# Moving the first weight sums from GpSimd to VectorE, and using four gathered experts before the second tile's norm

## The reference

```python
def first_block(...):                                    # DEPTH = 1
    proj = rms_norm(h, g_mix_pre) @ w_in                 # conv, pool, u, v, and three gates
    z_sgu, z_conv, z_pool, z_gate = jnp.split(proj, SPLITS, axis=-1)
    br_a = spatial_gating(gelu(z_sgu), ...) @ w_sgu_out  # layer_norm of v, then a mix over tokens
    br_b = conformer_conv(z_conv, ...) @ w_conv_out      # a * sigmoid(gate), 31 taps, layer_norm, silu
    br_c = multiscale_pool(z_pool, ...) @ w_pool_out
    gates = sigmoid(z_gate).reshape(bsz, s, 3, D_MODEL)
    merged = gates[:, :, 0] * br_a + gates[:, :, 1] * br_b + gates[:, :, 2] * br_c
    h = h + rms_norm(merged @ w_out, g_mix_post)
    ...                                                  # feed-forward layer, embedding gate

def second_block(...):
    for i in range(2):
        h = layer_norm_2(DN_ALPHA * h + mix(h), ln_mix_g[i], ln_mix_b[i])
        h = layer_norm_2(DN_ALPHA * h + peer_ffn(h, ...), ln_ffn_g[i], ln_ffn_b[i])

def peer_ffn(x, w_q, sub_keys, u, v):                    # 128 tokens at a time
    q = (xb @ w_q).reshape(128, 8, 2, 128)               # 8 heads
    s1, i1 = lax.top_k(q . sub_keys[:, 0], 16)
    s2, i2 = lax.top_k(q . sub_keys[:, 1], 16)
    top_s, pos = lax.top_k(s1[:, None] + s2[None, :], 16)
    eidx = (i1 * 128 + i2) at pos                        # 16 experts per token and head
    h = gelu(einsum('thkd,td->thk', u[eidx], xb))
    return einsum('thk,thkd->td', softmax(top_s) * h, v[eidx])
```

## Time and profile before

| what | value |
|---|---|
| median of 3 runs | 2305.41 us (2303.39 to 2305.59) |
| the profiled execution's own time | 2303.99 us |
| its span | 2302.3 us |
| PE busy | 2074.8 us, 90% of the span |
| DVE busy | 1433.8 us, 62% |
| ACT busy | 697.5 us, 31% |
| POOL busy | 725.1 us, 31% |
| bytes moved | 703.05 MB |

### The profile page before, as it was taken

The page is one execution under the profiler, slowest core; times in us unless marked ns, Lnnn a source line. Parts: engine busy times, 40 slices in busy tenths (PEclk is TensorE's granted clock), DMA queues, the critical chain, the costliest instruction groups (busy, mean ns, idle before and its releaser), DMA issues.

```text
span 2302.3 us, 21846 instructions
## 1 busy us (share of the span) xinstructions
PE 2074.8 (90%) x6098; PEld 1096.2 (48%) x6098; DVE 1433.8 (62%) x3220; ACT 697.5 (30%) x1511; POOL 725.1 (31%) x641
## 2 busy tenths in 40 slices
PE   9989999999999999999887787889999989777876
PEld 8854455454876655444332222367544534222222
DVE  3997757675363336666666666532666666666664
ACT  1112102110200214334443434424334344343442
POOL 0274340000000004445544444400244544444442
PEclk9999999999999999999999999999999999999999
DMA  5434443444445249999999999973699999999997
GB/s 227 146 128 166 163 156 132 174 169 167 182 151 222 85 156 388 422 421 421 422 421 422 422 422 422 421 289 103 257 421 422 421 421 422 421 422 422 422 422 323
DMA packets 98441, 703.05 MB, mean 305 GB/s; under 512 B 11136, under 2 KB 11648, under 8 KB 13248
## 3 DMA queue, kind: packets, MB, share of 16 engines
q0 software_dynamic: 73856, 537.17, 56.2%
q1 hardware_dynamic: 20880, 147.33, 17.6%
q10 hardware_dynamic: 3632, 17.63, 2.1%
HBM read 700.51 MB, written 1.05 MB: 305 GB/s over the span
## 4 chain that ended last, share of the span: by engine, by line
PE 42%; DMA 30%; ACT 5%; issue 5%; DVE 3%; POOL 1%; POOLq 0%; DVEq 0%; ACTq 0%
DMA arena<-uv,expert_index 30%; PE aux L978 12%; PE acc L556 10%; PE acc L521 6%; PE aux L521 4%; PE aux L831 4%; PE acc L901 2%; PE acc L988 1%; ACT arena L1511 1%; ACT arena L1514 1%; ACT L1511 1%; POOL arena L1247 1%; ACT L1503 1%; DVE arena L2220 1%; PE acc L878 0%
## 5 line engine op out<-in xcount | busy, mean ns | idle before, releaser
L978 PE MATMUL aux<-arena 128*128 128x512 f32 x2048 | 1006.1, 620 | 186.0 <-ACT arena L1514 181.7
L1247 POOL DMA_INDIRECT arena<-uv,expert_index x512 | 589.2, 1151 | 1000.1 <-PE aux L978 612.2
L2220 DVE SCALAR_TENSOR_TENSOR arena<-arena 128x1024 f32<-128x1024 f32 x512 | 634.1, 1239 | 425.5 <-DMA arena<-uv,expert_index 424.9
L978 PEld LDWEIGHTS aux<-arena 128*128 128x128 f32 x2048 | 366.3, 192 | 725.5 <-ACT arena L1514 438.8
L1511 ACT ACTIVATE arena<-ident,dots 128x128 f32<-128x128 f32 x512 | 205.2, 401 | 702.8 <-DVE arena L2220 700.3
L556 PE MATMUL acc<-x,w_ring 128*128 128x256 f32 x1264 | 277.4, 382 | 5.1 <-DVEq L1957 2.7
L556 PEld LDWEIGHTS acc<-x,w_ring 128*128 128x128 f32 x1264 | 241.8, 192 | 39.6 <-issue 3.4
L1514 ACT ACTIVATE arena<-arena,gate 128x128 f32<-128x128 f32 x512 | 205.5, 401 | 17.0
L1743 DVE TENSOR_TENSOR first_query_weights<-w_ring 128x1024 f32<-128x1024 f32 (+1 forms) x63 | 76.1, 1207 | 106.3 <-PE aux L521 102.2
L521 PE MATMUL acc<-first_query_weights,arena 128*128 128x512 f32 (+1 forms) x268 | 133.4, 580 | 0.0
L1719 DVE SCALAR_TENSOR_TENSOR arena<-arena,channel_vectors x240 | 115.4, 562 | 0.2
(11 more groups left out here) (328 smaller groups left out, 1846.5 us busy)
## 6 DMA issues: line engine op xcount, KB each, us to landing
w_ring<-stream SPq DMA_DIRECT2D x139, 1024.0 KB, 4.8
arena<-uv,expert_index POOLq DMA_INDIRECT x512, 14.8
first_query_weights<-first_heads ACTq DMA_DIRECT2D x4, 1024.0 KB, 8.5
row_vectors<-rows ACTq DMA_DIRECT2D x3, 1024.0 KB, 12.4
scratch<-keys ACTq DMA_DIRECT2D x2, 1024.0 KB, 6.3
arena<-ret_out_held ACTq DMA_DIRECT2D x2, 1024.0 KB, 15.4
x<-first_heads ACTq DMA_DIRECT2D x2, 1024.0 KB, 4.8
arena<-rows ACTq DMA_DIRECT2D x1, 1024.0 KB, 4.7
```

The lines of the kernel that those rows point to most:

```text
L978: last = nc.tensor.matmul(AUX[2 * tt + c][:, :], DG[:, slot, :], G[:, row(slot), D + c * 512:D + (c + 1) * 512], start=False, stop=closes)
L1247: pool.indirect_dma_start(G[:, row(s), :], None, uv, bass.IndirectOffsetOnAxis(ap=EIDX[:, par, s:s + 1], axis=0),).then_inc(gathered[s % R ...
L2220: v.scalar_tensor_tensor(G[:, row(slot), 0:D], G[:, row(slot), 0:D], 1.0, HTM[:, tt, :], ALU.mult, ALU.mult, accum_out=HD[:, slot:slot + 1 ...
```

## The change

It has three parts.

1. In the first block the weight sums of unit 0 go from POOL to DVE. The last two rounds of taps are no longer a loop; in the last round three `combine(0, j)` stand before tap 8, 16 and 24, and the fourth stands behind it. POOL makes the sums of the normed input (`split(X1, ...)`) before its pooling work instead of after it, in another region (63 in place of 17), and no longer makes weight sums. Its sums of the pooled branch wait for unit 0's four steps, and those of the convolution go to a region of their own (17). The first `norm_values` goes from ahead of `combine(1, 0)` to behind `combine(1, 3)`, the second to behind `combine(BRANCH, 1)`. In the last merge one part of four stays on POOL and three are DVE's (two and two before).
2. In both expert layers four slots (`FIRST`) of the first unit are used ahead: DVE makes their dots before `mixer_norm(1)`, ACT their weights before the root of that norm, PE their products before the third head's early query. Places of `G` are given anew. In layer 1 seven gathers need no wait for the projection. In layer 0 the gathers 4, 5 and 6 wait for a part of it each (`rows_left`), and the order of that projection is turned round so that those parts come first; the weight slots of the blocks 113 and 114 are given back later in it. The next searches' pieces are spread over the twelve slots that are left, two a slot at first.
3. In layer 0 the fourth head's query weights (1 MB) come by an ACT transfer into tiles 72 to 79 (`Q3W`), after the retention's last heads are scaled, and no longer by the stream, which is one block shorter; its query steps stand two a slot behind slots 4 to 7.

```diff
+FIRST = 4
-          ... ("peer_q0", 5),
+          ... ("peer_q0", 4),
-        def row(s):
-            return (s + 2) % RING
+        def row(layer, s):
+            return s if layer else (2, 3, 4, 5, 7, 0, 1, 6)[s]
...
 @@ PE, seven_step
-                        if unit:
-                            pe.wait_ge(combined, step - STEPS + 1)
-                        else:
-                            pe.wait_ge(combined_pool, step + 1)
+                        pe.wait_ge(combined, step + 1)
 @@ PE, peer
+                        if kt == 16 and (c, k) in ((1, 15), (0, 3), (0, 7)):
+                            last.then_inc(rows_left, 1)
+                        elif not rest:
+                            last.then_inc(projected, 1)
...
+                if kt == 16:
+                    last.then_inc(w_free[(base + 1) % SLOTS], 1)
+                for s in range(FIRST):
+                    weigh_slot(layer, 0, s, layer * (PEER_SLOTS + 1) + 1 + s + 1)
                 pe.wait_ge(third_loaded, 16 * (layer + 1))
...
-                 [(1, k) for k in range(2, 8)] + [(0, k) for k in range(8)] + [(1, k) for k in range(8, 16)])
+                 [(1, k) for k in range(8, 16)] + [(0, k) for k in range(8)] + [(1, k) for k in range(2, 8)])
 @@ POOL, gathers
-                            if par == 0 and s == RING // 2:
+                            if par == 0 and layer == 0 and 4 <= s < RING - 1:
+                                pool.wait_ge(rows_left, s - 3)
+                            if par == 0 and s == RING - 1:
                                 pool.wait_ge(projected, TT * (layer + 1))
 @@ ACT
             gain_heads(3)
+            act.dma_start(Q3W, first_heads[2 * EARLY]).then_inc(fourth_loaded, 16)
...
                 exps(0, units0 + 1, None)
+                for s in range(FIRST):
+                    slot_weights(0, s, None)
                 root(RT)
 @@ DVE, first block
+                for k in range(CONV):
+                    if k in between:
+                        chain.wait_back(0)
+                        combine(0, between[k])
...
-            with repeat(dve, 2, (chain, 2 * CONV)) as i:
-                taps(i * 2 + 4)
+            taps(4)
+            taps(6, {8: 0, 16: 1, 24: 2})
+            combine(0, 3)
 @@ DVE, peer
+                for s in range(FIRST):
+                    slot_dots(0, 0, s, None)
                 mixer_norm(1)
```

More of the change, by code:

```diff
@@ L996, in experts @@
                 for u in range(HEADS):
-                    for s in range(TOPK):
-                        weigh_slot(0, s, base + u * TOPK + s + 1, u == HEADS - 1 and s == TOPK - 1)
+                    for s in range(0 if u else FIRST, TOPK):
+                        weigh_slot(layer, 0, s, base + u * TOPK + s + 1, u == HEADS - 1 and s == TOPK - 1)
                         if 1 <= u <= HEADS - AHEAD and s == 2:
@@ L1003, in experts @@
                         if u < HEADS - AHEAD:
-                            for k in range(3) if u and s == 2 else () if u and s < 2 else (s,):
-                                query_step(k)
+                            two = 2 * (s - FIRST)
+                            for k in range(3) if u and s == 2 else () if u and s < 2 else \
+                                    (two, two + 1) if u == 0 and s < 2 * FIRST else (s,):
+                                query_step(k, layer == 0 and u == 0)
                         else:
@@ L1214, in _ @@
                 merge(1, *part)
-            for part in PARTS[:2]:
-                merge(2, *part)
+            merge(2, *PARTS[0])
             pool.wait_ge(input_ready, 4)
@@ L1350, in _ @@
             gates(2)
+            root(RT)
             for u in range(3):
@@ L1537, in peer @@
                 for unit in range(HEADS):
-                    for s in range(TOPK):
+                    for s in range(0 if unit else FIRST, TOPK):
                         slot_weights(unit, s, None)
-                        if s == 0:
+                        if s == (0 if unit else FIRST):
                             exps(1 - unit % 2, units0 + unit + 2, None)
@@ L1813, in _ @@
             add_gates(2)
-            for j in range(1, STEPS):
-                combine(BRANCH, j)
+            combine(BRANCH, 1)
+            norm_values(1)
+            combine(BRANCH, 2)
+            combine(BRANCH, 3)
             combine(BRANCH + 1, 0)
```

152 lines of the change are left out of this document (78 added, 74 removed).

## The result

The changed kernel takes **2291.38 us** (median of 5 runs, 2288.96 to 2294.75) against 2305.41 (5 runs, 2303.39 to 2306.95): ratio 0.994, 95% interval 0.9926 to 0.9955, 14.0 us less. Run again later it took 2291.79 against 2303.61 (ratio 0.9956, 0.9942 to 0.9969). It is faster, but 2284.0 was forecast, and 2291.4 lies above the range of 2281 to 2289. The profiled execution took 2291.38, its span 2289.7, so 12.6 us less than the span before.

The account below looks back on a forecast made before the run. It took PE (42% of the span) and gathers (30%) as the bounds; 15.2 + 0.5 + 5.0 = 20.7 us off 2303.99 gave 2283.3, and with the median 1.4 us above that execution it forecast 2284, range 2281 to 2289.

Parts of the forecast that it names:

- The first block, 15.2 us: Unit 0's weight sums on DVE: PE's 12.82 us pause goes, and 2.4 us of half clock after it.
- the cover that I counted on: First block: slack of later steps hides DVE's 1.1 us lateness, tightest 0.7 us; without it PE waits.
- The merge, 0.5: At the merge, the second pair of transposes can start at about 331.2 in place of 331.7: 0.5 us less.
- Its clock at 1.00: Sign of being right: full clock at the first product of `first_query_weights`, at about 162, with no pause before it.
- Layer 0's gathers, 5.0: Start of layer 0: transfer holes from 855 to 895, worth 5.1 us, close; 0.1 kept off, 5.0 us less.
- gathers 13 to 16 are late by 0.1 to 0.2 each: Layer 0: each slot there costs 2.58 us against the queue's 2.49, so these gathers slip 0.1 to 0.2 us each.
- slot 5 at 890: Layer 0: ACT's four tokens' copies and two table loads push slot 4 to 886 and slot 5 to 890.
- The fourth head's weights, 0: Layer 0: one block leaves the stream, but four blocks stand among the gathers before and after; nothing won.
- Layer 1, 0: Layer 1's start: transfers at 421 GB/s from 1640 to 1690 have no hole, so slots ahead bring 0.
- The partial refill (0.17): Rival, 0.17: ACT and PE pace slots 4 to 8; with slot 4 4 us later, 1 to 4 us stay; 2285 to 2288.
- Layer 1 lagged: Rival, 0.07: PE idles in layer 1, clock may fall to 0.50, gathers 12 to 16 2 to 5 us late; 2284 to 2288.

Follow-up runs that it names:

- both edits: Three kernels with slots ahead, query steps moved to slots 8 to 15 and unit 1's exponential before the root, in both layers or layer 0 alone: 2289.89, 2290.02, 2287.69 us.
- experiment 14: Kernel before plus the first block's part alone, with DVE's loops over layer 0's units written out: 2294.98 us, against 2290.30 without that.
- experiment 2: Kernel before plus only four slots ahead in both layers and the fourth head's weights by ACT transfer: 2303.82 us, ratio 1.0001.
- experiment 7: Changed kernel with query steps moved to slots 8 to 15 and unit 1's exponential ahead of the root, in both layers: 2289.89 us, ratio 0.9941.
- experiment 9: Kernel before plus the first block's part alone, but the merge's last products two on POOL and two on DVE as before: 2292.82 us, ratio 0.9949.

## Why the prediction was wrong

**The first block, 15.2 us: right.** The products on ones ahead of the merge start 14.9 us earlier (325.92 to 311.03). DVE was late nowhere; the cover that I counted on held, and was larger at tap 8 than counted (143.6 in place of 150.3).

**The merge, 0.5: right.** From there to the pairs it is 6.11 us in place of 6.70, 0.6.

**The half clock near 600: missing in the sum, the first step that failed.** "Its clock at 1.00" was forecast for the first step only. The wait of 2.67 us, which ends at 598.2, stood in the trace of before (2.66, at 613.7) with the clock at 1.00 behind it, and the sum took that over as it was. After all was moved ahead by 15.5 us, the clock fell there in the changed kernel's two profiles, and 1.5 us went: the first gather came 14.0 earlier, not 15.7.

**Layer 0's gathers, 5.0: the second.** Up to gather 12 the working was right: its place was to be free for an issue 36.3 us behind gather 0's, and it went out 36.9 behind; its bytes flowed 5 us earlier than before. Wrong was "gathers 13 to 16 are late by 0.1 to 0.2 each". Gather 13 went out 3.8 us behind gather 12, because ACT's two table loads and exponential stand between slots 4 and 5. The prediction had them, with slot 5 at 890, and did not carry them on: by its own numbers gather 13 goes out at 892 and its bytes flow at 894.6, 0.5 us behind the 894.1 at which gather 12 is through. And a gather that finds the queue empty costs more than the 0.1 us that issue times of 2.58 against 2.49 suggest: gathers 12 to 17 were issued 3.8, 2.6, 2.6, 2.7 and 2.1 apart and first moved bytes 2.9 to 3.3 apart. Together 2.5 us went back by gather 20, of which the kernels with both edits regained 2.2. One reading was off, without effect here: gather 0's first packet is at 853.6 and not at 854.3, so bytes flow 1.9 us behind an issue, not 2.6, and the queue began 0.7 earlier.

**The third failed step, a term that the sum had at nothing:** it counted in mean bytes per microsecond, as if the sixteen transfer engines ended together. The layer ends with the last of them: 2.4 us won at gather 20 were 2.0 on fifteen engines and 0.8 at the last byte. Why the sixteenth falls behind in the changed kernel is argued from experiment 14, not shown.

**The fourth head's weights, 0.** Not tested apart; experiment 2, which has them, shows nothing either way.

**Layer 1, 0: right within what can be told.** 0.3 us by the means of fourteen profiles. The places were late (gather 20 at 59.0 in place of 58.2 us), but the end was not.

**The sum.** Forecast: 15.7 to the first gather, 5.0 in layer 0, nothing after. (With the 1.4 us to the median that is 2284.7, not 2284.) On average over the profiles: 15.5 - 1.5 to the first gather, 0.8 in layer 0, -0.3 in layer 1, together 14.5; the medians have 14.0 and 11.8, the spans 12.6. What the spans lack of 14.5 differs between executions of one kernel: 6.8 us of half clock between the layers in place of 3.4, and 1.5 us in layer 1.

**The rivals.** The partial refill (0.17) was the nearest mechanism: ACT and PE did pace the slots, and 2.5 of the 5 us were lost. Its condition was not met as it stands, since slot 4 was 0.6 us late and not 4; the loss came between slots 4 and 8. Its own 2285 to 2288 would have stood but for the half clock and the last engine. Layer 1 lagged hardly: PE waited 2.33 and 2.62 us for the slots ahead, and the clock fell to 0.50 in its first 40 us in the profile after (at 1640.4, for 3.4 us) and in one of the other five profiles with slots ahead in layer 1 (experiment 7, at 1634.0), so in two of six. The range was too narrow because each of its cases held one loss; three came together, and two of them, the half clock near 600 and the last engine, had no case at all.

## What to carry to other kernels

A stretch that the transfers bound ends with its slowest transfer engine: read the end of the stretch for the share at which it runs out, and price every loop that is written out for its code fetches, since one 8 KB block can put one engine 0.95 us behind for the rest of the layer. Keep the queue from running dry: gathers issued 2.6 us apart into an empty queue first moved bytes 2.9 to 3.3 us apart, against 2.5 behind a full one. When a long wait goes away by moving work to another engine, look where the engine that waited now stands: POOL's 23 us went to another sum. Shifting a kernel in time can move where the clock falls: a wait of 2.7 us that was free before cost 1.3 to 1.5 us afterwards, and products on ones that just fit the wait take it back.

## What the runs showed of the hardware

- In all sixteen profiles one POOL sum that began some 2 us behind a round of sixty DVE taps, at 0.40 us each, was open for 22.96 to 23.69 us and ended 1.0 to 2.2 us behind the last of them. Beside the next round of the changed kernel it was the other way: POOL's sums took some 1.3 us each, and fourteen taps 18.4 us.
- Packets of 8 KB in the instruction queue that grew with DVE's code, 0.31 to 0.33 us each, stood some 2 us ahead of six steps of 0.71 to 0.98 us by which one transfer engine fell behind in one layer (experiment 14).
- The granted clock fell to 0.50 for 3.4 us behind a PE wait of 2.65 to 2.67 us (at 597 to 601, in ten profiles), of 2.08 us (at 317.5, experiment 9) and of 1.50 us (at 316.5, experiment 7), and did not behind the waits of 2.66 and 2.08 us of the kernel before, nor behind that of 2.66 us in experiment 9.
- The way between the layers is 128.0, 129.4 and 130.6 us with none, 3.4 and 6.8 us of half clock: 1.3 us for each 3.4.
